# The choice block of a two-layer PEER network: second tile's output projection spread between the query products, its gate and norm on ScalarE and GpSimd, top-16 choice by pairs of heads

## The chip, the cores and the metric

One core of a Trainium2 chip runs the whole program. The metric is the device time of one execution in microseconds (us); 0.2% of this kernel is 8.7 us. TensorE (PE) has its weight loads listed apart as PEld; VectorE is DVE, ScalarE is ACT, GpSimd is POOL, SyncE is SP. All data is float32.

## What is computed

A backbone of two layers over 256 context tokens and 512 latent tokens of width 1024. Each layer mixes tokens by attention, projects the result with an output matrix, adds it under a gate to the residual stream, norms and modulates the sum, and feeds it to a PEER mixer. The part that the change touches is this, for the tokens of one tile (128 tokens):

```python
x  = x + mx[2] * ox                                  # ox = attention output @ w_out; mx[2] is the gate
hx = modulate(rmsnorm(x, norm2[i]), mx[3], mx[4])    # h * (1 + scale) + shift

def peer(h, wq, sub_keys, u_tab, v_tab):
    q = (h @ wq).reshape(T, P_HEADS, 2, P_DKEY // 2)           # 8 heads x 2 halves = 16 queries of 128
    s = jnp.einsum("thpd,hpnd->thpn", q, sub_keys)             # 128 scores per query
    sv, si = lax.top_k(s, P_TOPK)                              # 16 best per half
    cand = (sv[:, :, 0, :, None] + sv[:, :, 1, None, :])       # 16 x 16 sums per head
    fv, fi = lax.top_k(cand, P_TOPK)                           # 16 experts per head
    gate = jax.nn.softmax(fv, axis=-1)
    ...                                                        # gather u,v rows of 128 experts per token,
                                                               # gelu(u . h) * gate, weighted sum of v
```

## The kernel before

Tokens are handled in tiles of 128; there are two context tiles and four latent tiles. The PEER part of a layer has two blocks.

**The choice block**, `first_choice` (L1612), runs once in each layer, for two tiles: the context tiles in layer 0, the first two latent tiles in layer 1. It does, in the order of TensorE's program: `turn` (L1684), transposes of the attention output of both tiles; `out` (L1692), the output projection of both tiles, per tile two halves of 512 columns with eight 128x512 products each (32 products, 64 instructions in the trace); `hturn(0)` (L1706), eight transposes of the first tile's normed rows; and then 32 units `query(u)` (L1713, eight 128x128 products) each followed by `score(u-1)` (L1724). Units 0 to 15 are the 16 half heads of the first tile, units 16 to 31 those of the second. `hturn(1)` stands behind unit 8 (`HTURN`).

Beside it ScalarE copies the transposed rows to SBUF (L1750), takes the sum of squares and its root (`root`, L1753), and copies each query (L1763) and each score (L1768) out of PSUM. VectorE gates and adds the projection (`gated`, L1794), builds the norm (`norm`, L1801) for both tiles, and then makes the choice for the **first tile only**: for groups of four half heads `top16` (L1546: maximum of 8, their indices, replacement, maximum, indices), the 16 x 16 sums of two heads (L1842) and `top16` over them, then `expert_numbers` (L1568). The scores of the second tile are kept for the next block. SyncE loads the query weights (576 KB each, L1650) into a ring of four buffers: load u waits for `score(u-4)`.

GpSimd waits until `chosen`, then issues the indirect gathers of slots 0 to 5 (`EARLY`), and those of slots 6 and 7 only when all 32 scores are done, because three of the four buffers for query weights lie in slots 6 and 7 of the same ring. The block ends for all engines together (L1652).

**The expert block**, `run_experts` (L2621), is one loop over slots, 128 slots for each tile: 768 in layer 0, 512 in layer 1. A slot is a gather of 128 rows of 8 KB (1 MB) into a ring of eight (L1607), a product with a row sum on VectorE (L2812), three ScalarE instructions (L2831, L2833, L2837) and two 128x512 products on TensorE (L2848). The gather of slot n waits until the products of slot n-8 are done (`spent`). Attention and projections of the later tiles are woven between the slots.

## Time and profile before

| | us |
|---|---|
| median of 3 runs | 4360.94 |
| lowest and highest run | 4359.24, 4367.72 |
| the profiled execution | 4354.59 |
| its span | 4353.3 |
| mean granted TensorE clock in it | 0.961 of full speed |

The span is that of the records; the profiled execution lasted 1.3 us longer, and lies 6.3 us below the median of the runs. Times in the rows count from the start of the span. In layer 0 the choice block runs from about 374 to 488 us and the expert block from there to about 2.6 ms; in layer 1 the choice block runs from about 2901 to 3013 us and the expert block from there to the end.

### The profile page before, as it was taken

To read this page: it belongs to the slowest core of one execution; us is meant where nothing else is said; L and a number is where in the kernel's file an instruction comes from. 1 tells how busy PE (TensorE), PEld (TensorE's weight loads), DVE (VectorE), ACT (ScalarE), POOL (GpSimd) and SP (SyncE) were. 2 spreads that over 40 slices of the span, in tenths; PEclk is the share of its full clock that TensorE was granted. 3 is DMA by queue.
4 is the path that set the end of the run, shared out by engine and by line. 5 is a ranking of instruction groups with operands and counts; after the bars stand their busy time and mean duration, and the time that the engine had idled before them with its cause. 6 is when DMAs were issued, how large, how long until landed. Compare 5 with 4: busy or idle time off the path is not lost. (4 is left out here: it accounts for less than half of the span.)

```text
span 4353.3 us, 44433 instructions
## 1 busy us (share of the span) xinstructions
PE 3749.3 (86%) x12678; PEld 1911.6 (44%) x12678; DVE 2599.6 (60%) x5659; ACT 1749.8 (40%) x5145; POOL 1705.2 (39%) x1350
## 2 busy tenths in 40 slices
PE   5998889999998999878989966688999997777787
PEld 2345544555554445434444433556444552222222
DVE  3534787667866755676644433336875557766544
ACT  1123355555554444443333322423663433333333
POOL 0100244334445443445444422001444434556675
PEclk8999999999999999999999988799999999999999
DMA  4454899999999999999999971028999999999998
GB/s 177 155 228 176 338 419 407 405 422 425 400 423 422 423 425 426 427 390 427 427 427 427 426 302 55 4 80 295 426 403 426 424 423 399 427 427 427 427 427 364
DMA packets 248571, 1562.73 MB, mean 359 GB/s; under 512 B 30851, under 2 KB 44963, under 8 KB 77190
## 3 DMA queue, kind: packets, MB, share of 16 engines
q0 software_dynamic: 185088, 1342.36, 73.7%
q1 hardware_dynamic: 61014, 213.99, 13.0%
q10 hardware_dynamic: 2224, 3.55, 0.2%
q8 instruction: 101, 1.65, 0.1%
q14 instruction: 144, 1.18, 0.1%
HBM read 1551.43 MB, written 8.36 MB: 358 GB/s over the span
## 5 line engine op out<-in xcount | busy, mean ns | idle before, releaser
L2848 PE MATMUL ps<-ring,ex_diag 128*128 128x512 f32 x5120 | 2481.2, 619 | 405.1 <-ACT ex_diag L2837 379.2
L1607 POOL DMA_INDIRECT ring<-in_p_uv,expert x1280 | 1649.7, 1289 | 2144.5 <-PE ps L2848 1418.4
L2812 DVE SCALAR_TENSOR_TENSOR ring<-ring,H 128x1024 f32<-128x1024 f32 x1280 | 1558.3, 1225 | 1083.4 <-DMA ring<-in_p_uv,expert 1069.0
L2848 PEld LDWEIGHTS ps<-ring,ex_diag 128*128 128x128 f32 x5120 | 926.1, 194 | 1644.4 <-ACT ex_diag L2837 820.5
L2831 ACT ACTIVATE ex_act_w<-ex_dots 128x1 f32<-128x1 f32 x1280 | 258.0, 202 | 1461.3 <-DVE ring L2812 1456.3
L2837 ACT ACTIVATE ex_diag<-ident_sb,ex_weight 128x128 f32<-128x128 f32 x1280 | 514.0, 402 | 92.4 <-issue 4.1
L2833 ACT ACTIVATE ex_weight<-ex_act_w,gates 128x1 f32<-128x1 f32 x1280 | 377.0, 295 | 90.7 <-issue 3.5
L532 PE MATMUL ps<-win_w,hT 128*128 128x512 f32 (+1 forms) x480 | 190.3, 553 | 1.6 <-PEq L283 1.4
L532 PEld LDWEIGHTS ps<-win_w,hT 128*128 128x128 f32 x480 | 89.7, 190 | 103.4 <-issue 101.1
L1970 PEld LDWEIGHTS ps<-hTc,bs_w 128*128 128x128 f32 x768 | 110.8, 191 | 29.5 <-issue 23.7
L1970 PE MATMUL ps<-hTc,bs_w 128*128 128x128 f32 (+1 forms) x768 | 120.3, 310 | 0.3 <-issue 0.3
L2812 DVE DVE_READ_ACCUMULATOR ring<-ring,H 128x1 f32 x1280 | 105.8, 83 | 0.0
L2831 ACT ACT_TABLE_LOAD x72 | 92.4, 1283 | 1.9 <-PEq L1652 0.6
L547 ACT ACTIVATE ph_sq<-ps 128x512 f32<-128x512 f32 (+1 forms) x24 | 12.4, 517 | 163.3 <-PE ps L532 163.3
L766 PEld LDWEIGHTS ps<-KV,bs_probsT 128*128 128x128 f32 x480 | 63.1, 192 | 24.4 <-issue 24.4
L577 DVE TENSOR_REDUCE ph_ss<-ph_sq 128x8 f32<-128x512 f32 (+1 forms) x24 | 14.1, 586 | 99.1 <-ACT ph_sq L547 99.1
L837 DVE TENSOR_REDUCE bs_top<-ps 128x2 f32<-128x1536 f32 (+2 forms) x32 | 49.9, 1558 | 37.0 <-PE ps L790 35.5
L853 ACT COPY bs_probsT<-ps 128x512 f32<-128x512 f32 (+1 forms) x72 | 36.8, 511 | 86.7 <-PE ps L778 86.7
L2115 PEld LDWEIGHTS ps<-bs_w,hTc 128*128 128x128 f32 x512 | 60.9, 192 | 11.5 <-issue 11.5
L1970 PE MATMUL ps<-K,bs_w 128*128 128x256 f32 x256 | 65.7, 379 | 0.0
L1152 POOL TENSOR_TENSOR K<-K,lt_kn 128x512 f32<-128x512 f32 x6 | 7.8, 1304 | 143.9 <-DVEq L1125 143.9
L766 PE MATMUL ps<-KV,bs_probsT 128*128 128x64 f32 (+1 forms) x480 | 63.2, 270 | 0.1
(462 smaller groups left out, 3367.6 us busy)
## 6 DMA issues: line engine op xcount, KB each, us to landing
bs_w<-in_p_wqk SPq DMA_DIRECT2D x64, 576.0 KB, 8.1
ring<-in_p_wqk SPq DMA_DIRECT2D x48, 576.0 KB, 4.8
ca_mod_w<-in_w_mod SPq DMA_DIRECT2D x24, 1024.0 KB, 13.3
ring<-in_p_uv,expert POOLq DMA_INDIRECT x1280, 13.9
win_mod_w<-in_w_mod SPq DMA_DIRECT2D x16, 1024.0 KB, 4.9
bs_w<-in_e_w_out_tiles SPq DMA_DIRECT2D x24, 512.0 KB, 8.4
win_w<-in_e_w_in SPq DMA_DIRECT2D x9, 1024.0 KB, 9.2
fc_w_q<-in_p_wqk SPq DMA_DIRECT2D x16, 576.0 KB, 4.8
```

What stands on the lines that cost most here:

```text
L532: mm = pe.matmul(m.ps[:, u % 4, 0:halves * 256], m.hT[:, k, t * P:(t + 1) * P], pre.w[:, n % 2, 0:halves, k, :], start=(k == 0), stop=(k = ...
L766: mm = pe.matmul(self.O[:, cols], self.probsT[:, r % 2, x * P:(x + 1) * P], KV[:, self.blocks(n)[j], vals], start=(j == 0), stop=(j == las ...
L837: dve.tensor_reduce(self.top[:, n % 2, :], self.S[:, :, 0:w], AX.X, ALU.max)
L853: act.copy(self.probsT[:, r % 2, 0:wide], self.T[:, 0:wide]).then_inc(self.copied, 1)
L1607: pool.indirect_dma_start(m.ring[:, r, :], None, a["p_uv"], bass.IndirectOffsetOnAxis(ap=m.expert[:, t % 2, slot % SLOTS:slot % SLOTS + 1] ...
L1970: mm = pe.matmul(m.ps[:, self.q_banks[u % nq], 0:cols], w[:, j * P:(j + 1) * P], self.turned_of(self.tiles_of(u), j), start=(j == 0), stop ...
L2115: mm = pe.matmul(m.ps[:, 7, at:at + P], self.hT[:, k, i * P:(i + 1) * P], w[:, k * P:(k + 1) * P], start=(k == 0), stop=(k == KC - 1), ski ...
L2812: dve.scalar_tensor_tensor(out=ring[:, r, 0:D], in0=ring[:, r, 0:D], scalar=1.0, in1=h_of(t + t0), op0=ALU.mult, op1=ALU.mult, accum_out=d ...
L2831: act.activation(act_w[:, b:b + 1], dots[:, t % 2, n:n + 1], ACT.Gelu)
L2833: act.activation(weight[:, b:b + 1], act_w[:, b:b + 1], ACT.Copy, scale=gates[:, t % 2, n:n + 1])
L2837: act.activation(diag[:, b, :], m.ident[:, :], ACT.Copy, scale=weight[:, b:b + 1]).then_inc(diag_ready, 1)
L2848: mm = pe.matmul(mix_banks(t)[:, half, :], diag[:, b, :], ring[:, r, D + half * BANK:D + (half + 1) * BANK], start=(n == 0), stop=(n == SL ...
```

## The change

The output projection of the second tile is no longer one piece ahead of the queries. Its left half (8 products) stays there, its right half is spread, one product behind each of units 2 to 9. It goes to PSUM banks 2 and 3, no longer 6 and 7. ScalarE copies each half out of PSUM (`copy_mix`), GpSimd multiplies it by the gate and adds it to the residual stream; ScalarE takes the root at unit 12; VectorE takes only the reciprocal, between two groups of its choice; GpSimd then makes the normed rows in three passes over 1024 columns. `hturn(1)` moves from unit 8 to behind unit 15, and `score(15)` goes ahead of it. The choice on VectorE goes by two half heads (one head) at a time, eight groups where there were four. The exponential for the gates moves from unit 26 to unit 24. The same is done in both layers. `root` writes its squares into the rows of H, and `sq` becomes `mixed`.

```diff
-    HTURN, EXP_AT = 8, 26
+    PIECE_AT, MIX_AT, ROOT_AT, INVERT_AT, EXP_AT = 2, 10, 12, 10, 24
...
             def _(pool):
+                second, h = m.R[:, tiles[1], :], h_of(tiles[1])
+                pool.wait_ge(gate_loaded, 16)
+                for half in range(2):
+                    c = slice(half * BANK, (half + 1) * BANK)
+                    pool.wait_ge(mix_copied, half + 1)
+                    pool.tensor_tensor(mixed[:, c], mixed[:, c], gate[:, c], ALU.mult)
+                    pool.drain()
+                    pool.tensor_tensor(second[:, c], second[:, c], mixed[:, c], ALU.add).then_inc(mix_added, 1)
+                pool.wait_ge(inverted, 1)
+                pool.tensor_scalar(h, second, ss[:, 1:2], None, ALU.mult)
+                pool.drain()
+                pool.wait_ge(scale_ready, 1)
+                pool.tensor_tensor(h, h, scale[:, :], ALU.mult)
+                pool.drain()
+                pool.tensor_tensor(h, h, shift_row[:, :], ALU.add).then_inc(h_ready, 1)
                 pool.wait_ge(out_done, 4)
                 pool.wait_ge(chosen, 1)
...
-                for n in range(2):
-                    out(n)
+                out_first()
+                for k in range(KC):
+                    out_second(0, k)
                 hturn(0)
                 for u in range(NU):
                     query(u)
-                    if u:
+                    if u and u != NH:
                         score(u - 1)
-                    if u == HTURN:
+                    if PIECE_AT <= u < PIECE_AT + KC:
+                        out_second(1, u - PIECE_AT)
+                    if u == NH - 1:
+                        score(u)
                         hturn(1)
...
+                def copy_mix(half):
+                    act.wait_ge(out_done, 3 + half)
+                    act.copy(mixed[:, half * BANK:(half + 1) * BANK], m.ps[:, 2 + half, :]).then_inc(mix_copied, 1)
...
                 root(0)
+                copy_mix(0)
                 copy_turned(0, h_turned, h_copied, 0)
-                root(1)
                 for u in range(NU):
+                    if u == MIX_AT:
+                        copy_mix(1)
+                    if u == ROOT_AT:
+                        root(1)
                     query(u)
...
-                norm(0)
-                gated(1, 0, BANK, 3)
-                gated(1, BANK, D, 4)
-                norm(1)
-                for h in range(0, NH, 4):
-                    dve.wait_ge(taken, h + 4)
+                norm()
+                for h in range(0, NH, 2):
+                    if h == INVERT_AT:
+                        dve.wait_ge(rooted, 2)
+                        dve.reciprocal(ss[:, 1:2], ss[:, 1:2]).then_inc(inverted, 1)
+                    dve.wait_ge(taken, h + 2)
                     dve.sem_inc(claimed, 1)
-                    for _ in top16(dve, range(h, h + 4), m.val, sc, rest, m.pos):
+                    for _ in top16(dve, range(h, h + 2), m.val, sc, rest, m.pos):
                         pass
```

TensorE in layer 0 before, from the transposes of the attention output to unit 3 (`Qc` the attention output, `ring` with `hTc` 128x512 the projection, `ident_sb,H` is `hturn`, `hTc,ring` or `hTc,fc_w_q` 128x128 a query, `fc_qT` a score; xN counts products):

```order
136 L1688 MATMUL ps<-ident_sb,Qc 128x128 x16
137 L1701 MATMUL ps<-ring,hTc 128x512 x32
138 L1709 MATMUL ps<-ident_sb,H 128x128 x8
139 L1720 MATMUL ps<-hTc,ring 128x128 x16
140 L1730 MATMUL ps<-ring,fc_qT 128x128
141 L1720 MATMUL ps<-hTc,ring 128x128 x8
142 L1730 MATMUL ps<-ring,fc_qT 128x128
143 L1720 MATMUL ps<-hTc,fc_w_q 128x128 x8
```

The same place after, and then units 14 and 15 with the second `hturn`:

```order
136 L1704 MATMUL ps<-ident_sb,Qc 128x128 x16
137 L1713 MATMUL ps<-ring,hTc 128x512 x16
138 L1721 MATMUL ps<-ring,hTc 128x512 x8
139 L1731 MATMUL ps<-ident_sb,H 128x128 x8
140 L1742 MATMUL ps<-hTc,ring 128x128 x16
141 L1750 MATMUL ps<-ring,fc_qT 128x128
142 L1742 MATMUL ps<-hTc,ring 128x128 x8
143 L1750 MATMUL ps<-ring,fc_qT 128x128
144 L1721 MATMUL ps<-ring,hTc 128x512
...
177 L1750 MATMUL ps<-ring,fc_qT 128x128
178 L1750 MATMUL ps<-fc_w_q,fc_qT 128x128
179 L1731 MATMUL ps<-ident_sb,H 128x128 x8
180 L1742 MATMUL ps<-hTc,ring 128x128 x16
```

Eight of the 32 wide products have left the run ahead of `hturn(0)` and stand one by one behind the scores; two scores now stand directly ahead of the second `hturn`.

VectorE in layer 0 before, from the first tile's norm to the first group of its choice:

```order
284 L1809 TENSOR_TENSOR H<-H,fc_shift_row 128x1024
285 L1797 TENSOR_TENSOR ps<-ps,fc_gate 128x512
286 L1799 TENSOR_TENSOR R<-R,ps 128x512
287 L1797 TENSOR_TENSOR ps<-ps,fc_gate 128x512
288 L1799 TENSOR_TENSOR R<-R,ps 128x512
289 L1804 RECIPROCAL fc_ss<-fc_ss 128x1
290 L1806 SCALAR_TENSOR_TENSOR H<-R,fc_ss,fc_scale 128x1024
291 L1809 TENSOR_TENSOR H<-H,fc_shift_row 128x1024
292 L1549 MAX val<-fc_sc 128x8 x4
293 L1553 MAX_INDEX pos<-val,fc_sc 128x8 x4
```

After, the whole first group:

```order
284 L1845 TENSOR_TENSOR H<-H,fc_shift_row 128x1024
285 L1549 MAX val<-fc_sc 128x8 x2
286 L1553 MAX_INDEX pos<-val,fc_sc 128x8 x2
287 L1556 MATCH_REPLACE fc_rest<-val,fc_sc 128x128 x2
288 L1560 MAX val<-fc_rest 128x8 x2
289 L1563 MAX_INDEX pos<-val,fc_rest 128x8 x2
290 L1877 TENSOR_TENSOR fc_cand<-val 128x256
291 L1549 MAX best<-fc_cand 128x8
292 L1553 MAX_INDEX at<-best,fc_cand 128x8
293 L1556 MATCH_REPLACE fc_left<-best,fc_cand 128x256
294 L1560 MAX best<-fc_left 128x8
295 L1563 MAX_INDEX at<-best,fc_left 128x8
```

The seven instructions for the second tile are gone from VectorE, and every phase of a group has half as many instructions. GpSimd in layer 0 after, between the start of the block and the gathers (before, nothing stood there):

```order
30 L1680 TENSOR_TENSOR fc_mixed<-fc_mixed,fc_gate 128x512 [waits fc0_mix_copied,fc0_gate_loaded]
31 L1682 TENSOR_TENSOR R<-R,fc_mixed 128x512
32 L1680 TENSOR_TENSOR fc_mixed<-fc_mixed,fc_gate 128x512 [waits fc0_mix_copied]
33 L1682 TENSOR_TENSOR R<-R,fc_mixed 128x512
34 L1684 ISA
35 L1684 TENSOR_SCALAR H<-R,fc_ss 128x1024 [waits fc0_inverted]
36 L1687 TENSOR_TENSOR H<-H,fc_scale 128x1024 [waits fc0_scale_ready]
37 L1689 TENSOR_TENSOR H<-H,fc_shift_row 128x1024
38 L1607 DMA ring<-in_p_uv,expert 128x2048 [waits fc0_chosen,fc0_out_done]
```

Seven operations have come ahead of the gathers, and in layer 0 an `ISA` instruction with them, a change of GpSimd's code; the same kind of instruction stands at L630 in both kernels, and in layer 1 there is none.

## Rows read from the trace of the kernel before

**Rows 1.** Stretches: from:to, length, busy PE PEld DVE ACT POOL, clock, DMA share, GB/s.

```profile
423.00:483.00 60.00, 55.88 (x462) 52.94 (x463) 55.34 (x212) 14.84 (x53) 0.20 (x1) 1.00 0.77 252
483.00:488.00 5.00, 4.28 (x36) 3.90 (x35) 0.00 (x0) 1.24 (x5) 3.78 (x5) 1.00 0.72 249
488.00:540.00 52.00, 35.56 (x92) 15.55 (x93) 33.99 (x82) 25.06 (x63) 19.99 (x18) 0.94 1.01 420
540.00:620.00 80.00, 73.65 (x239) 37.39 (x238) 69.62 (x195) 44.86 (x126) 41.33 (x34) 0.98 1.01 427
3080.00:4300.00 1220.00, 1050.28 (x2644) 447.77 (x2642) 765.71 (x1590) 510.49 (x1563) 656.02 (x473) 0.99 1.01 422
```

**Rows 2.** Waits between 488 and 540 us: engine, line, releaser: us, times, longest.

```profile
DVE ring L2812 <- DMA ring<-in_p_uv,expert: 22.4, 12, 5.9
```

**Rows 3.** Timeline of TensorE, layer 0: start, us, what, [idle before <-releaser].

```profile
378.63 3.68 PE L1688 MATMUL ps<-ident_sb,Qc 128*128 128x128 f32 x16 [5.37 <-DVE Qc L1822]
382.10 28.22 PE L1701 MATMUL ps<-ring,hTc 128*128 128x512 f32 x64
410.16 1.04 PE L1709 MATMUL ps<-ident_sb,H 128*128 128x128 f32 x8
412.39 3.81 PE L1720 MATMUL ps<-hTc,ring 128*128 128x128 f32 x32 [1.19 <-ACT hTc L1750]
...
416.26 1.95 PE L1720 MATMUL ps<-hTc,ring 128*128 128x128 f32 x16
...
418.27 1.95 PE L1720 MATMUL ps<-hTc,fc_w_q 128*128 128x128 f32 x16
...
433.24 1.95 PE L1720 MATMUL ps<-hTc,ring 128*128 128x128 f32 x16
...
484.62 1.95 PE L1720 MATMUL ps<-hTc,fc_w_q 128*128 128x128 f32 x16
...
486.92 0.49 PE L1730 MATMUL ps<-fc_w_q,fc_qT 128*128 128x128 f32 x2
```

**Rows 4.** Timeline of VectorE, layer 0: norm, first group's phases, later steps, first slot.

```profile
403.21 1.23 DVE L1809 TENSOR_TENSOR H<-H,fc_shift_row 128x1024 f32<-128x1024 f32 x1
...
423.01 0.87 DVE L1549 MAX8 val<-fc_sc 128x8 f32<-128x128 f32 x4 [6.49 <-ACT fc_sc L1768]
423.96 0.09 DVE L1553 MATCH_VALUE_LOAD pos<-val,fc_sc 128x8 f32 x1
...
433.67 0.87 DVE L1549 MAX8 val<-fc_sc 128x8 f32<-128x128 f32 x4 [0.18 <-issue]
...
465.87 0.30 DVE L1570 CAST fc_posf<-pos 128x256 f32<-128x256 uint32 x1
...
481.69 0.23 DVE L1591 TENSOR_SCALAR expert<-fc_num 128x128 uint32<-128x128 f32 x1
...
488.61 1.23 DVE L2812 SCALAR_TENSOR_TENSOR ring<-ring,H 128x1024 f32<-128x1024 f32 x1 [5.87 <-DMA ring<-in_p_uv,expert]
```

**Rows 5.** Groups of VectorE, one group of the choice: line, shape, xcount | busy, mean ns | idle.

```profile
L1549 DVE MAX8 val<-fc_sc 128x8 f32<-128x128 f32 x4 | 0.9, 280 | 6.5 <-ACT fc_sc L1768 6.5
```

**Rows 6.** GpSimd, whole span, by shape; same columns.

```profile
L1152 POOL TENSOR_TENSOR K<-K,lt_kn 128x512 f32<-128x512 f32 x6 | 7.8, 1304 | 143.9 <-DVEq L1125 143.9
L1156 POOL TENSOR_TENSOR Qa<-Qa,lt_qn 128x768 f32<-128x768 f32 x2 | 4.0, 1993 | 0.0
```

**Rows 7.** Line L630: a record of GpSimd's sequencer, durations in ns, start in us.

```profile
L630 POOLq MODIFY_POOL_CONFIG  x2: 11/11/11, 71.1 to 71.1; - x2
```

**Rows 8.** Timeline of GpSimd: its first product, then gathers of both layers.

```profile
102.23 1.48 POOL L630 TENSOR_TENSOR ph_near<-KV,ph_cos 128x512 f32<-128x512 f32 x1 [66.18 <-DVEq L594]
...
482.80 1.02 POOL L1607 DMA_INDIRECT ring<-in_p_uv,expert  x1 [119.87 <-DVE expert L1591]
...
493.76 0.94 POOL L1607 DMA_INDIRECT ring<-in_p_uv,expert  x1 [0.56 <-issue]
...
3007.63 0.97 POOL L1607 DMA_INDIRECT ring<-in_p_uv,expert  x1 [288.45 <-DVE expert L1591]
```

**Rows 9.** DMA issues between 423 and 475 us: xcount, KB each, median us to landing.

```profile
ring<-in_p_wqk SPq DMA_DIRECT2D x16, 576.0 KB, 4.7
```

More of the change, by code:

```diff
@@ L1725, in score @@
                     pe.wait_ge(qT_ready, u + 1)
[L1726 to L1728 removed]
+                    if u >= 2:
                         pe.wait_ge(taken, u - 1)
@@ L1734, in _ @@
                     turn(n)
-                for n in range(2):
-                    out(n)
+                out_first()
+                for k in range(KC):
+                    out_second(0, k)
                 hturn(0)
@@ L1823, in _ @@
                 dve.wait_ge(gate_loaded, 16)
-                gated(0, 0, D, 2)
+                gated()
                 dve.wait_ge(vec_loaded, 16 * (4 if stream else 3))
```

77 lines of the change are left out of this document (41 added, 36 removed).

## The prediction

> **What bounds the kernel now.** I read three views first: the busy time by stretch, the waits in the first slots of the expert block, and the timeline of the choice block. The stretches [rows 1] show two different machines. In the expert block the DMA share is 1.01 and 420 to 427 GB/s flow, from 488 us on and through 1220 us of layer 1: that block is a stream of 1 MB gathers that fills the DMA engines. In the choice block only 252 GB/s flow (share 0.77), and while the first gathers start up, 483 to 488, no more than 249. So a choice block matters in two ways: when it lets the gather stream begin, and how many bytes are still owed when it begins. VectorE waits 22.4 us for gathers in the first 52 us of the expert block [rows 2]: there the slot loop has slack against its data.
>
> Two chains run through a choice block. TensorE's goes through projection, transposes and 32 units to 487.4 us, where all engines change blocks [rows 3]. VectorE's goes through the groups of the choice, 423.0 to 465.9, and the expert numbers to 481.9 [rows 4]; this one releases the first gather, issued at 482.8 and at work as slot 0 at 488.6 [rows 4, 8], 5.8 us later.
>
> **TensorE, step by step (layer 0).** A wide product costs 28.22 / 32 = 0.88 us [rows 3]. The first tile's 16 are unchanged, so its normed rows are ready as before at 403.21 + 1.23 = 404.4 [rows 4]. TensorE, now through 24 products by 382.1 + 21.2 = 403.3, waits for them and starts `hturn(0)` at 404.5, not 410.16: unit 0 starts 5.7 us earlier, at 406.7, and unit 2 at 410.6. A unit without a stall takes 2.01 us (416.26 to 418.27); 412.39 to 416.26 is two queries and the first score, 3.87. Over units 9 to 31 the mean is (484.62 - 433.24) / 22 = 2.34; the 0.33 on top is the wait for weights, whose load takes 4.7 us [rows 9] from a point two units back. Units 2 to 9 carry one wide product each and take 2.01 + 0.88 = 2.89, which covers the load; unit 10 starts at 410.6 + 8 x 2.89 = 433.7. So the eight moved products cost only 0.55 each, 4.4 us, against 7.1 saved ahead. Units 10 to 15, with a ring that is full at first, take about 2.2 each, and `score(15)`, which waits for its own query's copy (0.5: the block's last score starts 2.30 after its query at 484.62, a plain unit's 1.8 later), ends at 447.4.
>
> **GpSimd and what it holds.** The right half is complete at 433.7; copy 0.6, two passes of 1.30 [rows 6]: 437.0. The root at unit 12 lies inside ScalarE's idle time and ends near 440. VectorE comes to the reciprocal at its own fifth boundary, at 444.1 (below), so GpSimd starts the norm at 444.4. From 512 columns (1.304) to 768 (1.993) the price rises 0.27 per 100 columns, so 2.68 at 1024 [rows 6]. A pass with one tensor and a scalar is in no row: at most 2.68 as with two tensors, at least about half, 1.3; I take 2.0, the middle. With gaps: 444.4 + 2.0 + 5.4 + 0.3 = 452.1. TensorE, done at 447.4, stands 4.7 us, and everything of the second tile is queued behind that wait; nothing covers the transposes and their copy now, 2.2 us (410.16 to 412.39). Unit 16 starts at 454.3; before it was 433.24 + 7 x 2.34 = 449.6. With four loads ready (0.9 saved) unit 31 starts at 488.5 and the block ends at 491.3, 3.9 later than before. A clock fallen to half in that wait, as in the transposes behind the 5.4 us of idle time at 378 (3.68 us for 16, where eight at full clock take 1.04), would add up to 2; the last loads share the DMA engines with gathers, which adds 2 or so. I put the end at 493.5, 6 late.
>
> **VectorE, step by step.** Its first group waited for `score(3)`, now for `score(1)`: two units less, 4.0, and 5.7 from above, so 413.3 in place of 423.0. But a pair costs more than half of four. The first phase shows it: four MAX8 of 280 ns each [rows 5] take 0.87 together, one each 0.20, yet the next phase starts 0.95 after the first [rows 4], 0.16 behind the last one's turn. Such tails follow nearly all of the 11 phases, and sum to 1.65 of the 10.66 us of a group (423.01 to 433.67). They are paid once for each group, so a pair takes (10.66 - 1.65) / 2 + 1.65 = 6.15. TensorE delivers a pair in 5.8 and later 4.7 us, so VectorE never starves. Eight pairs and the reciprocal (0.3) take 49.5 in place of 42.9: they end at 462.8, 3.1 earlier, and so do the expert numbers and the first gather: 479.7. The bounds: no tail at all gives 5.33, then fed at 5.8 for the first four, 8 us earlier; a tail as long as a whole MAX8 (0.28 for each of 11) gives 6.9 or so, and 3 us later than before. The fifth boundary is 413.3 + 5 x 6.15 = 444.1. The exponential at unit 24 (near 473) finds its input ready since 464: nothing.
>
> **The sum.** Of 5.8 us from issue to landing 2.5 are the transfer (1.05 MB at 427 GB/s), so data flow 3.3 after the issue: from 486.1 before, from 483.0 now. Before, no weights were owed at that point. Now TensorE is in unit 28 at 483.0, and the loads for units 30 and 31 are owed: 1.18 MB, 2.8 us at the same rate. Gain: 3.1 - 2.8 = 0.3 us. The block's late end costs nothing as long as the stream does not run dry: six gathers and two loads last until 483.0 + 7.5 / 0.427 = 500.5, and slots 6 and 7, issued at the end of the block, must flow by then, so the end may come up to 497. The slot loop starting 6 us late finds its data waiting and has 22.4 - 5.9 = 16.5 us of waits to make it up from. Layer 1 is the same block (gather at 3007.63 [rows 8]; slightly more gain in the projection, no change of GpSimd's code). Both layers: about 1 us gained. From 4354.59 to 4353.6 for the profiled execution, which lies 6.3 below the median: **4360** on the median, that is, no change.
>
> **Rivals.** A: the tails of a pair are hidden, as in the lower bound. The gather goes out 8 us earlier, at 474.8; GpSimd gets its reciprocal 2 earlier as well, so unit 16 starts at 452 or, with quick passes on GpSimd, at 449. At 478.1, when data flow, 1.7 to 2.5 loads are owed, 2.4 to 3.5 us. Gain 4.5 to 5.6 a layer: 4350 to 4352. For it: I read one phase's tail and took it over to the others, whose ends differ. Against: that 0.95 stands behind 0.87 also where nothing was waited for.
> The Trainium skill (VectorE: DVE Perf Modes, The DRAIN you can't avoid) says that a flush follows every VectorE operation whatever stands between them. By that rule a smaller group costs nothing more, and the time would be rival A's; the 0.20 us spacing of operations that last 0.28 [rows 5] speaks against it.
>
> B, slower: GpSimd's norm takes 14 us, not 8, by a slow pass or by its code being changed at that point, and TensorE stands 11 us at `hturn(1)`. The block then ends at 501 to 503. It decides from 497: beyond that the DMA engines run dry between the sixth and seventh gather, 4 to 6 us a layer, and nothing gives it back. Both layers: 4360 + 10 to 12 = 4371; in layer 0 alone, 4365, still no change. For it: a scalar pass is in no row. Against: the other sequencer record of a code change (71.1) lies 31 us ahead of the first product, which then took 1.48 in place of 1.30 [rows 7, 8]; here it is issued without a wait as soon as the sums are done, 437.0, 7.4 us ahead of its use.
> The Trainium skill (GPSIMD Engine Reference, 2.1 Instruction dispatch) puts a load of new code at about 6 us, unseen in the profile. By that figure, as an estimate, it would end at 443, just ahead of 444.4; no run here shows it.
>
> C: a chain moves in a way that is not worked out here; a few us either way.
>
> **Chances and range.** Forecast 0.62 (4356 to 4365), A 0.17, B 0.17, C 0.04. The range takes in A's and B's ends: 4350 to 4371. 0.2% of the time, about what can be told from no change, is 8.7 us: faster 0.17, same 0.63, slower 0.20.
>
> **What would show it.** First group of VectorE at 413.3; a pair in 6.15; first gather near 479.7; the norm's three passes 7.7 together; TensorE idle about 5 us behind `score(15)`; end of the block at 491 to 495; DMA share 1.0 without a gap from 483. Wrong if a pair takes under 5.7 or over 6.6, or if the block ends beyond 497, or if a gap in the DMA appears behind the sixth gather.

## The result, and the profile after

| | before | after |
|---|---|---|
| median of 10 runs each, us | 4360.27 | 4376.84 |
| lowest and highest run | 4354.96, 4367.72 | 4368.58, 4385.7 |
| the profiled execution | 4354.59 | 4376.31 |
| its span | 4353.3 | 4375.0 |
| mean granted TensorE clock in it | 0.961 | 0.964 |

The ratio is 1.004, with a 95% interval of 1.0032 to 1.0049: slower by 16.6 us, where 4360 (4350 to 4371) was forecast. The time lies outside the range and on the side that had a chance of 0.20. The same kernel once more, beside the runs of the experiments, gave 1.0037 (1.0024 to 1.0051); what was expected of that run:

> The changed kernel again, beside the other three. All theories: ratio to the kernel before as measured first, 1.0032 to 1.0049, some 4375 to 4381; in its trace TensorE in unit 25 when the first gather goes out and the block end at 128 us or later from the block's start.

The choice block of layer 0 starts 4.4 us later in the profiled execution of after than in that of before (first transposes at 383.01, not 378.63). This start lies between 378.6 and 387.0 in all sixteen traces of this study, whatever the kernel, so I count times in the block from its own start and write them as +102.4.

TensorE after, layer 0, from the last score of the first tile to the end of the block (start, us, what, [idle before <-releaser]); it answers to [rows 3]:

```profile
451.94 0.49 PE L1750 MATMUL ps<-fc_w_q,fc_qT 128*128 128x128 f32 x2
457.87 1.97 PE L1731 MATMUL ps<-ident_sb,H 128*128 128x128 f32 x8 [5.45 <-POOL H L1689]
460.99 6.52 PE L1742 MATMUL ps<-hTc,ring 128*128 128x128 f32 x32 [1.15 <-issue]
...
484.51 0.39 PE L1750 MATMUL ps<-fc_w_q,fc_qT 128*128 128x128 f32 x2
...
486.52 0.39 PE L1750 MATMUL ps<-ring,fc_qT 128*128 128x128 f32 x2
...
488.75 1.95 PE L1742 MATMUL ps<-hTc,fc_w_q 128*128 128x128 f32 x16
...
496.58 3.78 PE L1742 MATMUL ps<-hTc,ring 128*128 128x128 f32 x16 [5.66 <-DMA ring<-in_p_wqk]
500.16 0.63 PE L1750 MATMUL ps<-fc_w_q,fc_qT 128*128 128x128 f32 x2
...
504.29 2.05 PE L1742 MATMUL ps<-hTc,ring 128*128 128x128 f32 x16 [1.42 <-DMA ring<-in_p_wqk]
...
510.19 3.03 PE L1742 MATMUL ps<-hTc,fc_w_q 128*128 128x128 f32 x16 [3.62 <-DMA fc_w_q<-in_p_wqk]
...
513.57 0.80 PE L1750 MATMUL ps<-fc_w_q,fc_qT 128*128 128x128 f32 x2
```

The wait for the second tile's normed rows is there, 5.45 us. Behind it TensorE works at half speed for some 9 us: eight transposes take 1.97 us, not 1.04, and the queries of units 16 and 17 take 6.52, not 3.81. At the end three units (28, 30 and 31) wait for weights, 10.7 us together, and the clock falls once more: 0.50 from 496 to 500 us, behind the wait of 5.66 us, where the query of unit 28 takes 3.78 us and not 1.95. The last score ends at 514.4, that is +131.4; before it ended at +108.8.

GpSimd after, layer 0: the norm, then the gathers of slots 0, 5, 6 and 7; it answers to [rows 8]:

```profile
449.76 2.85 POOL L1684 TENSOR_SCALAR H<-R,fc_ss 128x1024 f32<-128x1024 f32 x1 [7.97 <-DVE fc_ss L1871]
452.75 2.58 POOL L1687 TENSOR_TENSOR H<-H,fc_scale 128x1024 f32<-128x1024 f32 x1
455.47 2.34 POOL L1689 TENSOR_TENSOR H<-H,fc_shift_row 128x1024 f32<-128x1024 f32 x1
485.41 1.05 POOL L1607 DMA_INDIRECT ring<-in_p_uv,expert  x1 [27.59 <-DVE expert L1591]
...
491.75 0.94 POOL L1607 DMA_INDIRECT ring<-in_p_uv,expert  x1 [0.31 <-issue]
514.64 0.94 POOL L1607 DMA_INDIRECT ring<-in_p_uv,expert  x1 [21.96 <-PE ps L1750]
515.88 1.19 POOL L1607 DMA_INDIRECT ring<-in_p_uv,expert  x1 [0.30 <-issue]
```

The first gather leaves at +102.4, where it was +104.2: VectorE's chain gained 1.8 us. But slot 6 follows 23 us behind slot 5. What that does to the stream shows in the stretches of after, layer 0 and one of layer 1 (from:to, length, busy PE PEld DVE ACT POOL, clock, DMA share, GB/s); it answers to [rows 1]:

```profile
458.00:464.00 6.00, 4.85 (x22) 4.48 (x23) 5.18 (x25) 1.01 (x1) 0.00 (x0) 0.50 0.01 3
468.00:480.00 12.00, 11.30 (x99) 10.92 (x98) 11.44 (x11) 2.48 (x11) 0.00 (x0) 1.00 0.76 245
490.00:540.00 50.00, 34.29 (x136) 22.11 (x136) 18.54 (x40) 18.61 (x52) 14.67 (x14) 0.86 0.88 348
540.00:620.00 80.00, 70.05 (x215) 34.39 (x213) 70.31 (x203) 44.11 (x118) 36.91 (x31) 0.96 1.01 423
3080.00:4300.00 1220.00, 1051.28 (x2677) 451.86 (x2677) 774.62 (x1633) 517.67 (x1577) 648.74 (x473) 0.99 1.01 422
```

Once the stream is steady it flows as before (422 GB/s in layer 1). The granted clock is 0.50 from 458 to 464, the 1.2 GHz level, right behind the 5.45 us in which TensorE did nothing; and the DMA share from 490 to 540 us is 0.88, where [rows 1] has 1.01 from 488 to 540. The rate of the DMA engines from 500 to 520 us, in 40 slices of 0.5 us, shows the hole itself:

```profile
GB/s 463 410 412 424 427 432 428 426 441 433 417 395 386 435 414 457 421 435 353 328 213 98 66 33 16 33 0 0 0 0 0 0 164 180 262 328 459 426 361 262
```

From 510 to 516 hardly anything moves. In the issues between 480 and 520 us the weight loads show why TensorE came so late:

```profile
ring<-in_p_wqk SPq DMA_DIRECT2D x4, 576.0 KB, 9.9
```

They land 9.9 us after their issue (a median), where [rows 9] has 4.7. The same trace holds both: five loads into the ring issued between 470 and 485.4 us, ahead of the first gather, have a median of 4.9, the three behind it 10.3.

**One yardstick.** How much the DMA engines have moved in the first 170 us from the block's start says how far the stream has come. Before, 51.51 MB in layer 0 and 50.77 in layer 1; after, 45.81 and 47.59. The 8.88 MB missing are 20.8 us at 427 GB/s. From the start of the block in layer 0 to the end the trace of after is 17.3 us longer (the spans differ by 21.7, but 4.4 of that lie ahead of the block, where nothing was changed), and 16.6 lie between the medians. The rest of the program behind the block's start in layer 1 takes 1452.6 us before and 1459.2 after: 6.6 longer, with 3.18 MB, 7.4 us, missing.

### The profile page after: what moved, and what is told of

Same layout as the page of the kernel before. It is cut to its first block and busy times, and to the rows that moved or that the text cites. A ratio compares the mean times of both kernels' runs of the same rounds, so it can differ in the third digit from the quotient of the medians.

```text
span 4375.0 us, 44543 instructions
## 1 busy us (share of the span) xinstructions
PE 3747.6 (86%) x12678; PEld 1915.3 (44%) x12678; DVE 2595.6 (59%) x5655; ACT 1751.1 (40%) x5149; POOL 1729.4 (40%) x1364
## 5 line engine op out<-in xcount | busy, mean ns | idle before, releaser
L1794 ACT COPY fc_qT<-ps 128x128 f32<-128x128 f32 x64 | 17.0, 266 | 143.1 <-PE ps L1742 138.8
```

## The experiments

My theory after the result: TensorE's idle wait drops its clock; so it is two units late when the gathers go out; the weight loads it still needs then land at half the pace; each gates a unit, whose score gates the load four later; so the block ends late, slots 6 and 7 come late, and the DMA engines run dry. The rivals: pairs in the choice cost something by themselves; GpSimd's work, or the change of its code, is the price; the late end of the block costs by itself, through TensorE or VectorE.

Each kernel was timed beside the kernel before on the same chip. Most times in the expectations are for a kernel before of some 4360 us; it had 4366.56 beside e1 to e4 and 4363.16 beside e5 to e8, so I hold them against the ratio times 4360. All values but the ratio come from one profiled execution; "end" and "gather" count from the block's start, "unit" is the one under way on TensorE when the first gather goes out; a pair of values is layer 0 / layer 1; "rest" is the span behind the block's start in layer 1.

| run | ratio (95%) | gather | unit | end | MB in 170 us | rest |
|---|---|---|---|---|---|---|
| before | 1 | 104.2 / 106.9 | 30 / 30 | 108.8 / 112.0 | 51.51 / 50.77 | 1452.6 |
| after | 1.004 (1.0032 to 1.0049) | 102.4 / 104.0 | 25 / 25 | 131.4 / 128.7 | 45.81 / 47.59 | 1459.2 |
| after_again | 1.0037 (1.0024 to 1.0051) | 102.9 / 103.9 | 25 / 25 | 129.1 / 126.9 | 46.88 / 48.38 | 1459.6 |
| e1 | 1.002 (1.0008 to 1.0032) | 110.1 / 111.7 | 29 / 29 | 117.7 / 118.9 | 48.51 / 48.37 | 1460.6 |
| e2 | 0.9999 (0.9989 to 1.0009) | 104.7 / 103.4 | 29 / 26 | 110.9 / 123.2 | 51.00 / 49.79 | 1457.7 |
| e3 | 0.9994 (0.9985 to 1.0003) | 104.9 / 106.2 | 29 / 29 | 112.6 / 112.6 | 50.70 / 50.93 | 1453.8 |
| e4 | 0.9998 (0.9988 to 1.0008) | 107.5 / 111.0 | 31 / 30 | 109.4 / 114.7 | 50.07 / 49.11 | 1456.4 |
| e5 | 1.0007 (0.9999 to 1.0016) | 105.4 / 105.4 | 27 / 26 | 124.7 / 124.7 | 48.74 / 49.16 | 1456.3 |
| e6 | 1.0007 (0.9999 to 1.0016) | 109.2 / 111.7 | 29 / 29 | 118.7 / 121.1 | 48.85 / 48.31 | 1456.7 |
| e7 | 1.0001 (0.9992 to 1.0009) | 102.4 / 104.0 | 27 / 27 | 120.9 / 123.2 | 50.43 / 49.79 | 1456.4 |
| e8 | 0.999 (0.998 to 0.9999) | 96.6 / 100.0 | 26 / 26 | 115.8 / 120.2 | 52.61 / 51.10 | 1451.6 |
| e9 | 0.9996 (0.9987 to 1.0005) | 105.1 / 106.6 | 29 / 30 | 112.8 / 113.8 | 50.82 / 50.86 | 1452.6 |
| e10 | 1.0002 (0.9993 to 1.0011) | 106.4 / 107.5 | 30 / 30 | 110.9 / 111.7 | 50.52 / 50.68 | 1451.8 |
| e11 | 1.0036 (1.0022 to 1.0049) | 101.3 / 103.9 | 25 / 26 | 124.0 / 126.1 | 49.03 / 48.69 | 1458.5 |
| e12 | 0.9994 (0.9984 to 1.0003) | 104.4 / 103.4 | 28 / 28 | 117.3 / 118.5 | 50.76 / 51.13 | 1451.2 |
| e13 | 1.001 (1.0001 to 1.0019) | 106.9 / 110.2 | 29 / 29 | 114.2 / 117.1 | 50.01 / 48.96 | 1458.4 |

One more value sorts these kernels: the time from the gather of slot 0 to that of slot 6, which the end of the block releases. It is 29.2 / 25.0 us in after, 26.5 / 23.2 in after_again and 23.0 / 22.4 in e11, the three at 1.0036 and more. In every other kernel it is at most 20.5 us, and none of them is above 1.002.

### e1: the gathers wait for the weight loads

After, and one line more on GpSimd: no gather before 28 scores are done, by when all weights have been asked for.

```diff
                 pool.wait_ge(out_done, 4)
                 pool.wait_ge(chosen, 1)
+                pool.wait_ge(scored, NU - 4)
```

> The changed kernel, with one wait more on GpSimd: the gathers of slots 0 to 5 wait until 28 scores are done, by when all 32 loads of query weights have been issued. Theory T (collision): in the changed kernel four to six query loads are still owed when the gathers start, these are served at a quarter of the DMA rate, the block ends 20 us late and slots 6 and 7 wait for that. Then a LATER first gather makes the kernel FASTER: block end about 12 to 18 us earlier in each layer than in the changed kernel, time 4364 to 4370 against about 4377. Rival G (the late gather is itself what costs, by whatever makes it late): the first gather goes 4 to 6 us later and the time rises by as much in each layer, 4385 to 4389.

Measured: 1.002 (4375.05, where the kernel before gave 4366.56 on this chip), or 4369 on 4360, inside theory T's range and far from rival G's. The first gather goes out 7.7 us later than in after (4 to 6 were expected), the block ends 13.7 and 9.8 us sooner, and half of the loss is gone. Its interval only just touches that of after (and overlaps that of the repeat), and they were not timed side by side, so the size of the gain is uncertain. The loads point the same way. In this trace, where they all go out ahead of the gathers, the issues between 480 and 520 us are:

```profile
ring<-in_p_wqk SPq DMA_DIRECT2D x3, 576.0 KB, 4.7
fc_w_q<-in_p_wqk SPq DMA_DIRECT2D x2, 576.0 KB, 5.2
```

With the same loads and gathers that start later, nothing lands late. So it is the gathers in flight that make a load take 9 to 11 us. The loss is not all gone, since the gathers now are late themselves.

### e2: after, with the choice in groups of four again

```diff
-    PIECE_AT, MIX_AT, ROOT_AT, INVERT_AT, EXP_AT = 2, 10, 12, 10, 24
+    PIECE_AT, MIX_AT, ROOT_AT, INVERT_AT, EXP_AT = 2, 10, 12, 8, 24
...
-                for h in range(0, NH, 2):
+                for h in range(0, NH, 4):
                     if h == INVERT_AT:
...
-                    dve.wait_ge(taken, h + 2)
+                    dve.wait_ge(taken, h + 4)
...
```

> The changed kernel with the choice by four half heads again (as before), the reciprocal for the second tile at the boundary of the second group. Theory T: the norm on GpSimd starts about 4 us earlier and the first gather about 2 us earlier, so TensorE's wait at the second transposes shrinks from 5.5 to about 2 us, one or two loads fewer are owed when the gathers start, and 3 to 5 us are won in each layer: 4367 to 4371. Rival P (the pairs themselves are the loss): all of it goes, 4358 to 4362. Rival G: only the 2 us of the gather, 4373.

Measured: 0.9999, the loss is gone. That missed theory T's 4367 to 4371 and met the number of rival P. The reciprocal now stands behind the second group of four, earlier than behind the fifth pair, and GpSimd's norm with it: in layer 0 `hturn(1)` waits 0.98 us, not 5.45 (about 2 were expected), and takes 1.09 us, the full clock. In layer 1 it still waits 3.01 us, and the clock falls:

```profile
2972.96 1.97 PE L1731 MATMUL ps<-ident_sb,H 128*128 128x128 f32 x8 [3.01 <-POOL H L1689]
2976.07 5.26 PE L1742 MATMUL ps<-hT,ring 128*128 128x128 f32 x32 [1.15 <-issue]
```

There the gathers meet unit 26 and the block ends at +123.2, yet slot 6 follows slot 0 after 20.1 us, and the time is that of before. GpSimd does the same work here. That alone left two readings: either pairs are dear, or the wait is.

### e4: the kernel before, with pairs alone

```diff
-                for h in range(0, NH, 4):
-                    dve.wait_ge(taken, h + 4)
+                for h in range(0, NH, 2):
+                    dve.wait_ge(taken, h + 2)
...
-                    for _ in top16(dve, range(h, h + 4), m.val, sc, rest, m.pos):
+                    for _ in top16(dve, range(h, h + 2), m.val, sc, rest, m.pos):
...
```

> The kernel before with the choice by pairs of half heads alone. VectorE starts its first group at about 419 in place of 423 and pays 6.2 us for each of eight pairs (the trace of the changed kernel: 6.21) in place of 10.66 for each of four groups, so it ends 2.3 us later. TensorE is untouched, so nothing is owed. Theory T: 2 us lost in each layer, 4363 to 4366. Rival P: 15 us or more, 4375. If pairs cost nothing, 4360.

Measured: 0.9998, so pairs are not the cause. Two starts of pairs on VectorE in its trace, layer 0:

```profile
429.39 0.49 DVE L1549 MAX8 val<-fc_sc 128x8 f32<-128x128 f32 x2 [0.18 <-issue]
435.60 0.49 DVE L1549 MAX8 val<-fc_sc 128x8 f32<-128x128 f32 x2 [0.18 <-issue]
```

They lie 6.21 us apart, as in after, where half a group of four would be 5.33. The first gather is 3.3 and 4.1 us later than before, and this costs nothing that the medians can tell: theory T's loss of some 4 us lies just outside the interval.

### e7: the wait stays, the idle time goes

After, with 48 transposes of the identity, whose result nobody reads, ahead of the wait for the second tile's rows.

```diff
-    keep = m.n2_scale[layer]
+    keep, IDLE = m.n2_scale[layer], 48
...
                 def hturn(n):
-                    pe.wait_ge(h_ready, n + 1)
                     if n == 1:
                         pe.wait_ge(mix_copied, 2)
+                        for k in range(IDLE):
+                            pe.transpose(m.ps[:, 2, (k % 4) * P:(k % 4 + 1) * P], m.ident[:, :], m.ident[:, :])
+                    pe.wait_ge(h_ready, n + 1)
```

> The changed kernel with 48 transposes of the identity on TensorE into a free bank, between the last score of the first tile and its wait for GpSimd's norm (about 5 us of extra work with no use, in the place of 5.5 us of idle time). The clock should then stay full, and units 16 and 17 take 3.8 us in place of 6.5. Theory T (collision): TensorE is 3 to 4 us further when the gathers start (unit 27 in place of 25), the block ends 5 to 10 us earlier in each layer, time 4364 to 4370. If the fallen clock does not matter because everything behind it waits for loads anyway: no change, 4377.

Measured: 1.0001 (0.9992 to 1.0009), which is better than theory T's 4364 to 4370. This is the run that decides. TensorE in its trace:

```profile
455.84 5.40 PE L1730 MATMUL ps<-ident_sb 128*128 128x128 f32 x48
461.53 1.09 PE L1733 MATMUL ps<-ident_sb,H 128*128 128x128 f32 x8 [0.28 <-POOL H L1689]
463.77 3.81 PE L1744 MATMUL ps<-hTc,ring 128*128 128x128 f32 x32 [1.15 <-issue]
```

GpSimd's norm is where it was, unit 16 starts only 0.8 us sooner (+77.1, not +78.0), and the first gather leaves at the same +102.4 and +104.0. What is gone is the slow stretch: 1.09 and 3.81 us, where after has 1.97 and 6.52. Its row of the stretch from 458 to 464 us says the same, clock 1.00:

```profile
458.00:464.00 6.00, 4.57 (x40) 4.12 (x39) 5.18 (x25) 1.01 (x1) 3.33 (x2) 1.00 0.31 117
```

So some 3.6 us of TensorE time, and nothing else, put the first gather against unit 27 instead of 25, moved the end of the block from +131.4 to +120.9, and brought back all that the medians can tell. The likely reason that more came back than the theory had said is that the block now ends in time: slot 6 follows slot 0 after 18.8 and 19.5 us, and from 491 to 520 us no slice of 1 us falls below 320 GB/s. By the ratios of e7 and of after with its repeat (not timed side by side) useless work made the kernel some 16 us faster. It also clears the pairs, GpSimd's passes and its change of code: all of them are still in this kernel.

### e9 and e3: the wait taken away in two other ways

e9 makes the second tile's norm on VectorE, behind its fifth pair, and leaves gate and sum on GpSimd.

```diff
-                pool.tensor_scalar(h, second, ss[:, 1:2], None, ALU.mult)
...
-                pool.tensor_tensor(h, h, shift_row[:, :], ALU.add).then_inc(h_ready, 1)
...
-                        dve.reciprocal(ss[:, 1:2], ss[:, 1:2]).then_inc(inverted, 1)
+                        dve.reciprocal(ss[:, 1:2], ss[:, 1:2])
+                        dve.drain()
+                        dve.scalar_tensor_tensor(out=h_of(tiles[1]), in0=m.R[:, tiles[1], :], scalar=ss[:, 1:2], in1=scale[:, :],
+                                                 op0=ALU.mult, op1=ALU.mult)
+                        dve.drain()
+                        dve.tensor_tensor(h_of(tiles[1]), h_of(tiles[1]), shift_row[:, :], ALU.add).then_inc(h_ready, 1)
```

> The changed kernel with the second tile's norm on VectorE, in two passes behind the fifth pair (2.7 us), in place of GpSimd's three (8.1 us). The gate and the sum stay on GpSimd. The rows are ready at 66 to 70 us from the block's start, just when TensorE comes: no idle time, no fallen clock, unit 16 at 71 to 74 in place of 78. The first gather goes 2.7 us LATER, 105. Theory T: TensorE is in unit 29 or beyond when it goes out, the block ends at 111 to 114, time within 4 us of the kernel before, so 12 to 18 us faster than the changed kernel. Rival G (a later gather costs): 5 us slower than the changed kernel.

e3 puts the right half's products two by two behind units 1 to 4, and all that hangs on them earlier.

```diff
-    PIECE_AT, MIX_AT, ROOT_AT, INVERT_AT, EXP_AT = 2, 10, 12, 10, 24
+    PIECE_AT, MIX_AT, ROOT_AT, INVERT_AT, EXP_AT = 1, 6, 8, 6, 24
...
-                    if PIECE_AT <= u < PIECE_AT + KC:
-                        out_second(1, u - PIECE_AT)
+                    if PIECE_AT <= u < PIECE_AT + KC // 2:
+                        out_second(1, 2 * (u - PIECE_AT))
+                        out_second(1, 2 * (u - PIECE_AT) + 1)
```

> The changed kernel with the right half of the second projection behind units 1 to 4, two products each, its copy at unit 6, the root at unit 8, the reciprocal behind the third pair. GpSimd's norm is then done some 8 us before TensorE wants it: no wait at the second transposes, no fallen clock behind it. The choice stays by pairs and the first gather stays where it is to 2 us. Theory T: unit 16 starts about 7 us earlier, at most two loads are owed when the gathers start, and the collision is gone: 4352 to 4360, so 17 to 25 us faster than the changed kernel. Rival P (pairs) and rival G (gather time): within 4 us of the changed kernel, 4373 to 4378.

Measured: 0.9996 and 0.9994, the same as before, both as theory T had it. The second `hturn` in e9, then in e3, from the timelines of TensorE:

```profile
454.49 1.04 PE L1724 MATMUL ps<-ident_sb,H 128*128 128x128 f32 x8
456.68 3.81 PE L1735 MATMUL ps<-hTc,ring 128*128 128x128 f32 x32 [1.15 <-issue]
```

```profile
456.85 1.04 PE L1731 MATMUL ps<-ident_sb,H 128*128 128x128 f32 x8
459.04 3.81 PE L1742 MATMUL ps<-hTc,ring 128*128 128x128 f32 x32 [1.15 <-issue]
```

No wait, the full clock, unit 29 or 30 at the first gather, the end at +112.6 to +113.8. In e3 GpSimd does everything that it does in after, only earlier, and `hturn(1)` finds its rows ready: the same work is free. Neither kernel beats the one before by more than the interval.

### e8: the first gathers sooner, in the kernel before

The expert numbers for one half are copied, not computed, so that the gathers fetch other experts and the result is another; it makes VectorE's chain 6.8 us shorter.

```diff
     for half in range(2):
+        if half == 1:
+            dve.tensor_copy(num[:, 1, :].rearrange("p (h k) -> p h k", k=TOPK), halves[:, :, 1, :])
+            dve.drain()
+            continue
```

> The kernel before with a shortened making of the expert numbers: the second half of the pair of keys is taken from the list of positions as it stands, without looking it up (so other experts are read for the first tile of each layer, as many and as widely spread; the output differs). The first gather goes out 6.8 us sooner, everything else is as before. Theory T: TensorE is then in unit 27, three loads owed, not in unit 30; the block ends 5 to 10 us LATER than before although nothing was added to it, and the time does not fall: 4360 to 4372 where the kernel before has 4361 to 4366. Rival G (the time follows the first gather): 13 us faster, 4348 to 4353.

Measured: 0.999 (0.998 to 0.9999), some 4 us faster. Neither forecast was met: theory T had said that the time does not fall, rival G that it falls by 13. The last score and the gathers of slots 0 and 6, layer 0:

```profile
498.60 0.49 PE L1734 MATMUL ps<-fc_w_q,fc_qT 128*128 128x128 f32 x2
```

```profile
479.90 1.02 POOL L1611 DMA_INDIRECT ring<-in_p_uv,expert  x1 [111.65 <-DVE expert L1595]
...
499.36 0.94 POOL L1611 DMA_INDIRECT ring<-in_p_uv,expert  x1 [12.20 <-PE ps L1734]
```

The block ends at +115.8 and +120.2, 7 to 8 us later than before, since the gathers now meet TensorE in unit 26. Yet the kernel is faster: slot 6 follows slot 0 after 19.5 us, and from 483 to 520 us no slice of 1 us falls below 295 GB/s. In after it is 29.2 us, and six slices of half a microsecond are empty. So an end of the block that is 7 to 8 us late costs nothing by itself; what counts is whether the DMA engines run dry before slot 6. It also tells roughly the worth of an early gather, since 7 to 8 us earlier in each layer bought 2 us a layer; how much of that is due to the other experts that are fetched is not shown.

### e5, e6, e10: nothing to win around it

e5 is after with groups of four and the right half's products two by two behind units 4 to 7; e6 is e5 with e1's wait; e10 is the kernel before with groups of 2, 4, 4, 4 and 2 half heads.

```diff
-    PIECE_AT, MIX_AT, ROOT_AT, INVERT_AT, EXP_AT = 2, 10, 12, 10, 24
+    PIECE_AT, MIX_AT, ROOT_AT, INVERT_AT, EXP_AT = 4, 8, 10, 8, 24
```

> The changed kernel, choice by four half heads, the right half of the second projection behind units 4 to 7, two products each, its copy at unit 8, root at unit 10, the reciprocal behind the second group. VectorE starts at 39 us from the block's start (44 before) and sends the first gather at about 99.5 (104.2 before), with TensorE in unit 27. No wait at the second transposes. Theory T: the early gathers meet three owed loads and the block ends at 112 to 118; time between -5 and +6 us of the kernel before. Rival G: 9 us faster than before.

> The same as the run before it, but the first gathers also wait until 28 scores are done (all loads issued). Theory T: the first gather at 101 to 103, block end at 107 to 110, data without a gap from then on: 2 to 4 us won in each layer against the kernel before, and faster than the version without the wait by up to 10 us in all. Rival G: slower than the version without the wait by the 2 to 3 us that the gathers are held in each layer.

```diff
-                for h in range(0, NH, 4):
-                    dve.wait_ge(taken, h + 4)
+                for h, size in ((0, 2), (2, 4), (6, 4), (10, 4), (14, 2)):
+                    dve.wait_ge(taken, h + size)
```

> The kernel before with groups of 2, 4, 4, 4 and 2 half heads on VectorE in place of 4, 4, 4, 4. The first group starts 4 us sooner and one more group is paid with 1.6 us: first gather about 102 us from the block's start in place of 104.2, TensorE in unit 29, block end at 109 to 111. Theory T: 1 to 2 us won in each layer, 2 to 4 in all. If unit 28 is the last one started by then, the block ends 5 us or more later and the gain is at most 1 us in all.

e5 missed in all but the time: its gather was to leave at +99.5, and left at +105.4, because the second group of four stood 4.3 us for scores that now lay behind the moved products. Nor did the wait at the second `hturn` vanish. It lasts 2.17 and 3.25 us (2.30 and 2.72 in e6), and the clock falls behind it in both layers; in e5, layer 0:

```profile
454.19 1.09 PE L1731 MATMUL ps<-ident_sb,H 128*128 128x128 f32 x8 [2.17 <-POOL H L1689]
456.43 6.62 PE L1742 MATMUL ps<-hTc,ring 128*128 128x128 f32 x32 [1.15 <-issue]
```

So a wait of 2.17 us costs units 16 and 17 as much (2.8 us) as the wait of 5.45 us in after (2.7). The gathers of e5 meet unit 27 or 26, slot 6 follows slot 0 after 19.5 us, and the kernel loses nothing that the medians can tell. e6 missed its gain of 2 to 4 us a layer. Both gave 1.0007: with TensorE in unit 26 or 27, holding the gathers back gives nothing, though it ends the block 4 to 6 us sooner. e10 missed as well (+106.4, not +102) and is the same as before, 1.0002. The small group at the start begins earlier, but the group behind it then stands 4.1 us for scores.

### e11: only three gathers first

After, where slots 3 to 5 wait until all weights have been asked for.

```diff
                 for slot in range(EARLY):
+                    if slot == 3:
+                        pool.wait_ge(scored, NU - 4)
                     gather(pool, m, a, slot, 0)
```

> The changed kernel with only three gathers (3 MB) going out when the experts are chosen, the other three held until 28 scores are done. Theory T (loads that are owed wait behind gathers): the gathers fill the DMA engines for 7 us and not for 15, the owed loads come through sooner, and the block ends 5 to 12 us earlier than in the changed kernel; time 4368 to 4375. If the loads are slow for another reason than the gathers in flight, block end and time stay.

Measured: 1.0036 (five runs), no gain, a miss. The block ends 7.4 and 2.6 us sooner, and 3.2 MB more have moved by 170 us in layer 0; 1200 us into layer 0, however, its stream is 4.22 MB behind that of before, as after's is (4.05). Where it loses the rest between the two points stays open.

### e12 and e13: combinations

e12 is e3 with groups of 2, 2, 2, 2, 4 and 4; e13 is e7 with e1's wait.

```diff
-                for h in range(0, NH, 2):
+                for h, size in ((0, 2), (2, 2), (4, 2), (6, 2), (8, 4), (12, 4)):
```

> The version with the early norm on GpSimd (right half behind units 1 to 4, root at unit 8) with groups of 2, 2, 2, 2, 4 and 4 half heads in place of eight pairs: two groups fewer are paid, 3.3 us. First gather at about 101.6 us from the block's start in layer 0 (104.9 with eight pairs, 104.2 before), unit 28 or 29 under way, block end at 112 to 116. Theory T: bytes come sooner by 1 to 3 us in each layer if unit 29 is under way, 4354 to 4360 where the kernel before has 4362; if only unit 28 or 27 is, the block ends at 118 or later and the time stays at that of the kernel before. Rival G (time follows the first gather alone): 5 to 7 us faster than before in both cases.

> The version with the 48 useless transposes and, as in the first experiment, gathers that wait until 28 scores are done. Theory T: the block then ends at 112 to 114 from its start in place of 121 to 123, but the first gather goes out 3 us later and the bytes that the DMA engines have moved by then are the same to 1 MB, so the time stays within 5 us of the version without the wait. If the late block end were what costs (slots 6 and 7, and the slot loop, start 8 us sooner), 8 to 16 us faster than that version.

e12 gave 0.9994 (0.9984 to 1.0003): its gathers leave at +104.4 and +103.4, later than forecast, but the best that can be said is that it is no slower. e13 gave 1.001 (1.0001 to 1.0019) where e7 had 1.0001 (0.9992 to 1.0009) on another chip: within 5 us of it, as theory T had said, and without the gain of 8 to 16 us that a costly late end would have given. The intervals overlap, so it is no better than e7 and may be worse. Of the three kernels that got e1's wait, only after, whose block ended latest, gained by it.

## Why the prediction was wrong, point by point

**Right.** Measured from the block's start, most of the forecast's steps came out. `hturn(0)` starts at +26.1 (forecast +25.9). The moved products cost what was said: unit 10 starts at +55.2 (+55.1). `score(15)` ends at +69.4 (+68.8). The first pair of the choice begins at +34.9 (+34.7) and a pair takes 6.21 us (6.15), as VectorE's starts of pairs in after show:

```profile
417.90 0.49 DVE L1549 MAX8 val<-fc_sc 128x8 f32<-128x128 f32 x2 [8.83 <-ACT fc_sc L1799]
...
430.70 0.49 DVE L1549 MAX8 val<-fc_sc 128x8 f32<-128x128 f32 x2 [0.18 <-issue]
...
436.91 0.49 DVE L1549 MAX8 val<-fc_sc 128x8 f32<-128x128 f32 x2 [0.18 <-issue]
```

That rules out rival A. The Trainium skill (VectorE: DVE Perf Modes, The DRAIN you can't avoid) says that a flush follows every operation; the same section adds that an operation which is not held starts earlier. Were there one flush for each operation and no more, a pair would cost half of four, 5.33; the 6.21 here speak against it. The first gather leaves at +102.4 (+101.1).

**GpSimd's norm, slightly under-sized.** The pass with a scalar takes 2.85 us: not the 2.0 taken, and above the upper bound of 2.68 that came from passes with two tensors. The three passes take 8.05 us (7.7 forecast), in layer 1 (2984.57 to 2992.6) as in layer 0, so the change of GpSimd's code, which only layer 0 has, cost nothing here. The rows are ready at +74.8 (+73.5), and TensorE stands 5.45 us (4.7).

**The clock, named but not carried on.** The prediction said that a clock fallen to half "would add up to 2". It took 0.93 us on the transposes and 2.71 on units 16 and 17, 3.6 together. I had sized it by the transposes at 378 [rows 3] alone and forgotten the units behind them. Of this term and the one for the shared DMA engines, 4 us together, the forecast end took only 2.2 (491.3 to 493.5). And I put the clock on the end of the block, where it could hide, not on the count of weight loads, where it could not. e7 shows that without it there is no loss.

**The step that failed.** "Now TensorE is in unit 28 at 483.0, and the loads for units 30 and 31 are owed." 483.0 is +104.4, where the forecast has the data begin to flow, 3.3 us behind the issue of the gather. At that distance from the block's start TensorE was in unit 26 (486.74 to 488.5). At the issue of the first gather itself (485.41) it was in unit 25, score 23 just behind it (484.51) and score 24 ahead (486.52), where the forecast's own steps give unit 27; the loads for units 28 to 31 were all still to come, so four and not two met the gathers. I priced owed loads by their bytes, 2.8 us, as if they only took their turn. That was wrong: the load for unit 28, free to go at 486.9 after its score, lets its unit start at 496.58; score 27, which stands right behind that query, ends at 500.8 and frees the last load only then, and it lands for 510.19. Two such rounds of almost 10 us follow one another in layer 0, because four buffers tie each load to the score of four units before; and the waits let the clock fall again, so that the queries of units 28 and 31 take 2.9 us more than at full clock. "... the last loads share the DMA engines with gathers, which adds 2 or so" is the term that was mis-sized: the block ended at +131.4, where +114.9 was forecast. e7 divides the 16.5 us, as far as two traces can: with unit 27 under way at the first gather, as the forecast's steps had it, the block still ends at +120.9. So 6.0 us belong to loads that land late even then, and cost nothing there, and 10.5 to the time at half clock. The table shows a steep step: with unit 29 to 31 under way at the first gather the block ends 2 to 10 us after it, with 28 (e12) 13 to 15, with 26 or 27 some 18 to 20 (22 in e11's layer 1), with 25 from 23 to 29.

**Rival B, right in its mechanism and wrong in its cause.** It asked for a norm of 14 us and got 8. But its breaking point, an end of the block beyond 497 (on before's scale; measured 510.0), is what was passed, and the gap in the DMA between slots 5 and 6 is what it said would follow. It gave 4371; the end lay further out, and the time was 4377. (Its own 4 to 6 us a layer make 8 to 12 in all, not the 10 to 12 that it added.) The slack of the slot loop was there and was used, as the waits of VectorE between 480 and 620 us in after show (engine, line, releaser: us, times, longest), where before has 30.1 us for gathers, 22.4 of it up to 540 [rows 2]:

```profile
DVE ring L2847 <- PEq L1653: 27.3, 1, 27.3
DVE ring L2847 <- DMA ring<-in_p_uv,expert: 12.0, 11, 2.5
```

But it only brings VectorE back to its data; bytes that did not move while the engines stood are not given back. The break point itself I had taken as comfortable, 497 against 493.5, without asking how steeply the end depends on what lay before it.

**What supports this, and what stays open.** In the traces of e1 to e13 the rest of the program in layer 1 follows the bytes moved in the block to within 3 us: e1 has 2.40 MB, 5.6 us, missing and is 8.0 longer; e7 2.3 and 3.8; e3 -0.4 and 1.2; e8 -0.8 and -1.0; e9 -0.2 and 0. One execution varies by as much, so for single microseconds this decides nothing. In layer 0 the fit is looser: from block to block the traces follow the bytes to within 6 us, but e11 is 15.4 us longer than before with 5.8 us of bytes missing, and e13 14.0 with 3.5. Shown by runs are the trigger (e7, and e9 and e3, each by another way) and that later gathers can pay (e1, with an interval that just touches that of after). That loads land late because gathers are in flight is shown by e1, which changes only the start of the gathers: 4.7 to 5.2 us there, 9.9 in after. By what means the gathers slow them (the share of the engines, the memory, the queues) stays open. e11 and the layer 0 of e13 are not explained.

## What to carry to other kernels

Ahead of a stream that fills the DMA engines, count which loads of the block before have been issued when it starts, not how many bytes they are: where each load is tied to progress by a ring, every round of the ring that falls behind the start takes the slow landing time in full (here two rounds of almost 10 us). Then ask how long the first transfers of the stream keep the engines busy; a late end of the block is free until then. A wait of 2 to 6 us on TensorE can cost more than its length, since the work behind it runs at half clock (here 3.6 us more); move what releases it (here the norm, a few units earlier) or, failing that, fill it with products that nobody reads. And when a step is priced at "up to 2" and taken as hidden, follow it to the next thing that is counted in whole units.

## What the runs showed of the hardware

- TensorE idle for 5.45 us (after): granted clock 0.50 (1.2 GHz) in the stretch behind it, back at 1.00 from 468 us. Idle for 0.98 us in the same place (e2, layer 0): no fall. Idle for 3.01 us (e2, layer 1): a fall, 1.97 and 5.26 us. Idle for 2.17 us (e5): the eight transposes behind it are still at full speed, 1.09 us, and the two queries behind them slow, 6.62. 48 transposes in its place (5.40 us at the full clock, e7): no fall.
- A load of 576 KB lands after 4.7 us beside other loads of weights and after 9 to 11 us when indirect gathers of 1 MB have started ahead of it: 10.3 in after, 9.0 in e8, 9.7 and 10.8 in e7. (The median of all loads in e7 from 480 to 520 us, 6.9, mixes loads from ahead of the first gather and behind it.)
- On GpSimd a pass over 128x1024 with one tensor and a scalar from memory took 2.85 us, longer than with two tensors (2.58 and 2.34).
- The Trainium skill (GPSIMD Engine Reference, 2.1 Instruction dispatch) puts a load of new code at about 6 us. No run here shows such a price: with the code changed some 8 us ahead of the next pass, that pass took 2.85 us, as in layer 1, where nothing was changed. A load of that length could have passed unseen in those 8 us, and no run issues the pass sooner.
